# A two-layer hybrid decoder trunk on one core: weight pieces of 2 MB in one transfer each, where there were two of 1 MB

## What is computed

```python
def hier_moe(h, wg, bg, we, be, w_gate, w_up, w_down):
    ...   # router: the best of 4 groups, then 2 of its 4 experts; combine holds their weights
    for e in range(N_EXPERTS):                       # 16
        y = (jax.nn.silu(t @ w_gate[e]) * (t @ w_up[e])) @ w_down[e]
        out = out + combine[:, e:e + 1] * y

def reference(x, ...):
    for layer in range(DEPTH):                       # 2
        h = rmsnorm(x, norm_mix[layer])
        y = even_mixer(h, ...) if layer % 2 == 0 else conv_mixer(h, ...)
        x = x + y
        h = rmsnorm(x, norm_ffn[layer])
        x = x + hier_moe(h, ...)
    return rmsnorm(x, norm_final)
```

## Time and profile before

| | |
|---|---|
| median of 3 runs | 1220.52 us (1220.33 to 1223.4) |
| profiled execution, its own time | 1219.09 us |
| its span, first to last instruction | 1217.3 us |
| mean granted TensorE clock | 0.939 |
| TensorE matmuls busy | 1093.8 us, 90% |
| VectorE busy | 873.7 us, 72% |
| ScalarE busy | 658.2 us, 54% |
| SyncE's transfer queue (q1) | 241.64 MB, 52.1% of 16 engines' span |

### The profile page before, as it was taken

One profiled execution on the slowest core, in us unless ns is written; L12 is line 12 of the kernel. 1 busy time (PEld: TensorE's weight loads), 2 busy tenths in 40 slices (PEclk: granted clock), 3 DMA queues, 4 the chain that ended last, 5 costly groups with the idle time before them and its releaser, 6 DMA issues.

```text
span 1217.3 us, 15272 instructions
## 1 busy us (share of the span) xinstructions
PE 1093.8 (90%) x5316; PEld 830.8 (68%) x5316; DVE 873.7 (72%) x1135; ACT 658.2 (54%) x811; POOL 108.8 (9%) x157
## 2 busy tenths in 40 slices
PE   5999995796999999999994599999999999999980
PEld 4776774475887777777773587887887777777750
DVE  5254555366478999999995645245779999999974
ACT  5133444344236888888883322213348888888851
POOL 2000000021010000000001300000100000000005
PEclk8999997798988999999997799999979999999995
DMA  8632222003218999999992833323159999999935
GB/s 300 183 128 69 79 78 69 18 1 136 72 69 290 388 398 406 402 397 401 409 413 93 323 104 101 107 69 107 62 203 366 396 394 407 402 394 400 419 148 207
DMA packets 78607, 286.36 MB, mean 235 GB/s; under 512 B 16631, under 2 KB 16631, under 8 KB 62172
## 3 DMA queue, kind: packets, MB, share of 16 engines
q1 hardware_dynamic: 66236, 241.64, 52.1%
q0 software_dynamic: 8592, 30.95, 7.7%
q10 hardware_dynamic: 3728, 13.11, 2.8%
HBM read 266.79 MB, written 20.20 MB: 236 GB/s over the span
## 4 chain that ended last, share of the span: by engine, by line
PE 86%; DVE 5%; ACT 3%; issue 2%; DMA 2%; POOL 1%; ACTq 0%; POOLq 0%; SPq 0%; DVEq 0%; PEldq 0%
PE ps L1478 26%; PE ps L1480 25%; PE ps L1479 25%; PE ps L1754 2%; PE ps L1460 1%; PE ps L1569 1%; PE ps L1615 1%; PE ps L1687 1%; DMA arena<-y_rows_dram,arena 1%; PE ps L1590 1%; ACT w_split L589 1%; PE ps L1708 1%; DVE arena L927 1%; DVE x_sb L1252 1%; PE ps L1778 1%
## 5 line engine op out<-in xcount | busy, mean ns | idle before, releaser
L906 DVE TENSOR_TENSOR w_split<-ring,w_split 128x1024 fp32r<-128x1024 f32 x452 | 540.2, 1220 | 81.8 <-ACT w_split L589 69.4
L589 ACT CAST w_split<-ring 128x1024 fp32r<-128x1024 f32 x452 | 472.6, 1052 | 214.9 <-PE ps L1480 211.7
L1478 PE MATMUL ps<-w_split,hT 128*96 128x512 f32 (+1 forms) x960 | 386.8, 403 | 11.4 <-DVE hT L1300 6.2
L1479 PE MATMUL ps<-w_split,hT 128*96 128x512 f32 (+1 forms) x960 | 380.3, 396 | 0.0
L1480 PE MATMUL ps<-w_split,hT 128*96 128x512 f32 (+1 forms) x960 | 380.2, 396 | 0.0
L1478 PEld LDWEIGHTS ps<-w_split,hT 128*96 128x96 f32 (+1 forms) x960 | 163.0, 170 | 71.6 <-DVE hT L1300 6.6
L1480 PEld LDWEIGHTS ps<-w_split,hT 128*96 128x96 f32 (+1 forms) x960 | 162.4, 169 | 62.2
L1479 PEld LDWEIGHTS ps<-w_split,hT 128*96 128x96 f32 (+1 forms) x960 | 163.1, 170 | 56.6
L1478 PE MATMUL ps<-hT,w_split 128*128 128x512 f32 (+1 forms) x384 | 146.4, 381 | 6.0 <-issue 4.1
L1480 PE MATMUL ps<-hT,w_split 128*128 128x512 f32 (+1 forms) x384 | 143.9, 375 | 0.0
L1479 PE MATMUL ps<-hT,w_split 128*128 128x512 f32 (+1 forms) x384 | 143.8, 375 | 0.0
(11 more groups left out here) (201 smaller groups left out, 861.0 us busy)
## 6 DMA issues: line engine op xcount, KB each, us to landing
ring<-in_exp_w_gate SPq DMA_DIRECT2D x64, 1024.0 KB, 11.0
ring<-in_exp_w_up SPq DMA_DIRECT2D x64, 1024.0 KB, 5.1
ring<-in_exp_w_down SPq DMA_DIRECT2D x64, 1024.0 KB, 11.2
ring<-in_w_in_even SPq DMA_DIRECT2D x14, 1024.0 KB, 12.1
y_rows_dram<-arena ACTq DMA_DIRECT2D x32, 384.0 KB, 6.9
ring<-in_w_in_odd SPq DMA_DIRECT2D x12, 1024.0 KB, 5.4
ring<-in_w_out_even SPq DMA_DIRECT2D x4, 1024.0 KB, 5.1
h_rows_dram<-arena POOLq DMA_DIRECT2D x8, 512.0 KB, 4.1
```

Of the source, the lines that this page charges most:

```text
L589: s.copy(hi_of(c), raw(c)).then_inc(hi_ready, 1)
L906: v.tensor_tensor(lo_of(c), raw(c), hi_of(c).bitcast(F32), ALU.subtract).then_inc(lo_ready, 1)
L1478: mm(out, a[0], b[0], start=start, stop=False)
L1479: mm(out, a[1], b[0], start=False, stop=False)
```

## The change

A piece is now loaded by one transfer of 2 MB into two neighbouring slots, and the two slots share one semaphore. The transfer waits until both slots have been used up. ScalarE's first cast of a piece waits for the whole piece.

```diff
-        slot_landed = [sem(f"slot_landed{i}") for i in range(RING)]
+        pair_landed = [sem(f"pair_landed{i}") for i in range(RING // 2)]
...
-                rows = src.shape[1] // 2
-                for half in range(2):
-                    n = 2 * piece + half
-                    if n >= RING:
-
-                        sp.wait_ge(lo_ready, plus(2 * (n - RING) + 2, i, 24))
-                    sp.dma_start(ring[:, n % RING, :].rearrange("p (k n) -> p k n", k=rows),
-                                 src[:, half * rows:(half + 1) * rows, :]).then_inc(slot_landed[n % RING], 16)
+                n = 2 * piece
+                if n >= RING:
+
+                    sp.wait_ge(lo_ready, plus(2 * (n - RING) + 4, i, 24))
+                sp.dma_start(ring[:, n % RING:n % RING + 2, :].rearrange("p s n -> p (s n)").rearrange(
+                                 "p (k n) -> p k n", k=src.shape[1]), src).then_inc(pair_landed[n % RING // 2], 16)
...
-                    act.wait_ge(slot_landed[n % RING], plus(16 * (n // RING + 1), i, 32))
+                    act.wait_ge(pair_landed[n % RING // 2], plus(16 * (n // RING + 1), i, 32))
```

## The result

The changed kernel takes 1237.9 us (median of 4 runs, 1233.4 to 1243.2), against 1220.4 us (median of 4) before. The ratio is 1.0145, with a 95% interval of 1.0113 to 1.0176: slower, by 17.5 us, outside of the range of 1218.5 to 1228. The profiled execution took 1243.16 us, with a span of 1241.4 us. It is the slowest of the four and its span is 24.1 us longer than the 1217.3 us of before, so the losses that its trace shows are larger than the median's.

The account below looks back on a forecast made before the run. TensorE was taken to set the pace in the experts, with transfers as slow within 1%. All terms were 0 us but the start's 0.4: 1220.5 + 0.4 = 1220.9 us on the median, no change, range 1218.5 to 1228.

Parts of the forecast that it names:

- One issue for two: On SyncE, half of the issues, about 0.4 us each, go away from an engine that only waits and issues: 0 us.
- The start: At kernel start the first cast waits for the whole pair, at about 15.8; cost 0.4 us, bounds 0 and 2.8 us.
- The ramp into the experts: Second gate's pair, issued at about 384.4, needed at 392.89: 8.5 us against 7.8 alone, so 0 us.
- The later issue: In the experts, first halves go out 3.2 to 3.7 us later; 0 us while two pairs stay in line.
- The later use: Experts' first casts wait for second halves: down 0.7 us late in layer 0, gate 1.5 in layer 1; 0 us.
- the 2.2 us in front of gate: Room between the subtraction behind gate's first casts, ending at 521.0, and the gate reading it at 523.22.
- The 4.5 us of room of a chunk: In the experts, a chunk's spare time after cast and subtraction, within the 7.3 us of five chunks.
- The rival of late casts: In the experts, pairs over 2.2 us late make gate wait: 1226 us with 2% of rate lost; chance 0.2.
- Longer runs block the small transfers: In the experts, doubled runs delay each gather by 2 us; if steps waited, 1 us each, 1250 us; chance 0.03.
- Larger transfers are worth something: 2 MB at once saves an estimated 2 us a piece; at layer ends 4 us, 1216.5 us at best; chance 0.04.

Follow-up runs that it names:

- e2: Kernel before plus both rules (issue when both slots are free, first cast waits for both halves), still two 1 MB transfers per piece: 1239.2 us, 1.0157.
- e12: Changed kernel with gathers from expert 3 of each layer on (counted from 0) replaced by reads of 16 rows of 128 bytes: 1235.2 us, 1.0141.

## Why the prediction was wrong

**One issue for two: 0 us.** Right as far as anything shows it: the version with both rules and two issues is not faster.

**The start: +0.4 us.** Right, and smaller. ScalarE and TensorE at the start of the kernel after:

```profile
15.59 1.99 ACT L587 CAST w_split<-ring 128x1024 fp32r<-128x1024 f32 x2 [2.93 <-DMA ring<-in_w_in_even]
```

```profile
18.04 0.77 PE L1476 MATMUL ps<-w_split,hT 128*128 128x512 f32 x1 [3.35 <-DVE w_split L904]
```

The first cast moved from 13.03 to 15.59 (15.8 forecast), the first product from 17.95 to 18.04. Its cost is 0.09 us.

**The ramp into the experts: 0 us.** Right for TensorE, though the prediction looked at the second gate only. The next down is the one that is late. ScalarE's first cast of it in the kernel after waits 2.47 us, and TensorE loses nothing by it up to 450 us (242 products before, 241 after); its loss begins behind that (191 products before, 180 after):

```profile
406.93 2.00 ACT L587 CAST w_split<-ring 128x1024 fp32r<-128x1024 f32 x2 [2.47 <-DMA ring<-in_exp_w_down]
```

```profile
400.00:450.00 50.00, 50.00 (x241) 35.61 (x240) 43.58 (x43) 36.62 (x44) 3.71 (x3) 1.00 1.02 391
450.00:490.00 40.00, 38.32 (x180) 26.75 (x179) 35.42 (x35) 30.49 (x37) 1.97 (x2) 1.00 1.01 380
```

In layer 1 it is the same: 191 products before and 193 after from 930 to 970 us, and a loss from there on. The lead of the ring lasts for two to three steps, and then the loss begins.

**The later issue: 0 us while the engines keep their rate.** This is the step that failed. The condition stood in the prediction, and I took it as met since two pairs would always be in line and the engines would never run dry. They hardly did: the share stayed at 1.01. But an engine that is never idle can still move less: 384 instead of 402 GB/s, with one gather beside the weights that cost 1.6 us of transfer instead of 0.6. With the late issue alone the rate did hold (402 GB/s in layer 0); with both rules it did not. The forecast counted the gather's bytes and not what its reading does to the weights, though every fall to 310 to 350 GB/s beside a gather could be read from the trace of before.

**The later use: 0.7 us of margin in layer 1.** It failed with it. Down in layer 0 was put at 0.7 us late; with the late use alone it waits 1.5 us on the mean (12.1 in 8) and up to 2.2 us, all of the lead already, and with the late issue alone 1.1 us on the mean, where none was forecast. Either alone costs nothing. I costed the two rules one after the other against the same lead, the 2.2 us in front of gate, and never their sum. Together they leave too little: waits of up to 3.2 us, and 17.5 us of time. (The 4.5 us of room of a chunk is 5.0 by the prediction's own terms, 7.3 - 1.05 - 1.22; nothing hangs on it.)

**The rival of late casts** named the right mechanism, its waits (gate for line 1293, which is L1291 now) and its point of decision, 0.3 us lost in a step. It was mis-sized: its upper bound of 5 us took 2% of rate over the last 10 steps of a layer; measured were 4.5% (402 to 384 GB/s) in layer 0 and 3.5% (400 to 386, from 930 to 1150 us) in layer 1, from the third or fourth step of each layer on, 16.7 us in the profiled execution. The 2% had no row behind it.

**Longer runs block the small transfers** was given 0.03 and 2 us a gather. The 2 us is what a gather's landing grew by (7.5 to 9.5), and no gather came too late for its own use, as argued. But the version with runs of 8 KB at most and both rules (e2) has gathers that land after 9.0 us by its DMA view, and a time of 1239.2 us, so the long runs are not needed for it.

**Larger transfers are worth something.** No sign of it. The Trainium skill (DMA: Bandwidth & Descriptors, "Rules for kernel authors") tells authors to coalesce many small transfers into a large one. At 1 MB these were not small, and here the merged transfer of 2 MB (1237.9 us) is as slow as the two of 1 MB under the same rules (1239.2 us).

**Shown and not shown.** Shown: both rules together cost the time and neither alone does; the kernel before has next to no DMA room to pay with; with the rules on down alone, nearly the whole loss comes from where the gather falls among the weights. In the changed kernel the profiled execution lost nearly all of its transfer time beside gathers, but that this is the cause there is argued from the trace: the later gather brings back the products of the later experts and not a clearly better time, and without the gathers' rows the median stays at 1235.2 us. Not shown: why the same rows cost more beside the end of up and the start of down than beside down or gate; why the later gather doesn't help from 970 to 1050 us in layer 1; and what the executions of e12 lose that were not profiled. That an empty line is a part of it was seen in a trace and not tested by itself.

## What to carry to other kernels

Merging two transfers into one also merges their buffers: the first half is asked for later and may be used later, and each of the two takes from the same lead. So check their sum against the smallest lead of the ring. Where transfers and products run within 1% of each other, the rate of DMA engines that are never idle is no constant. Read it in 1 us windows beside the small transfers of the kernel before, and ask where these will fall once the large ones shift. With the rules on down alone, holding back one small transfer by 2.9 us in each step took the ratio from 1.0093 to 1.0021, some 9 us. It did nothing in the kernel that had its lead, and in the changed kernel it made TensorE wait for that transfer, so look for its own deadline too.

## What the runs showed of the hardware

- DMA engines with a busy share of 1.0 moved 410 to 430 GB/s with no gather beside the weights, 311 to 348 GB/s beside a gather's rows in the kernel before, and 209 to 336 GB/s beside a gather's rows elsewhere among the weights, in the kernel after. There (507 to 510 us) a run of 16 KB took 0.87 to 1.14 us, against 0.61 us with no gather beside it. The Trainium skill (DMA: Bandwidth & Descriptors, "Queues, rings and completion order") states that each engine takes turns between its queues, packet by packet. That rows and weights both get slower fits with it; that their sum falls by half does not follow from it.
- Plain reads of 96 rows, on GpSimd's queue and on ScalarE's (1245.5 and 1246.9 us), cost no less than an indexed gather of 96 rows (1237.9 us).
